# Up and gate projections with both halves of x in one 512-column product, a bank per 128 channels

## What is computed

```python
def sq_relu_mlp(h, w1, w2):                      # D_FF = 4096
    z = jax.nn.relu(jnp.einsum('bsd,df->bsf', h, w1))
    return jnp.einsum('bsf,fd->bsd', z * z, w2)
...
h = h + sq_relu_mlp(rmsnorm(h, norm_mlp[layer]), mlp_w1[layer], mlp_w2[layer])
...
def swiglu(x, w_gate, w_up, w_down):             # D_FF_2 = 2816
    return (jax.nn.silu(x @ w_gate) * (x @ w_up)) @ w_down
...
h = h + 0.5 * swiglu(rms_norm(h, ffn1_norm[l]), ffn1_w_gate[l], ffn1_w_up[l], ffn1_w_down[l])
```

## Time and profile before

| | |
|---|---|
| median of 3 runs | 1067.23 us (1067.21 to 1068.12) |
| the profiled execution's own time | 1068.05 us |
| its span, first to last instruction | 1066.3 us |
| TensorE busy | 1030.0 us, 97% |
| VectorE busy | 673.1 us, 63% |
| ScalarE busy | 485.1 us, 45% |
| GpSimd busy | 68.7 us, 6% |
| granted TensorE clock, mean | 0.989 of full |
| HBM traffic | 173 GB/s |

### The profile page before, as it was taken

One profiled execution on the slowest core, in us unless ns is written; L12 is line 12 of the kernel. 1 busy time (PEld: TensorE's weight loads), 2 busy tenths in 40 slices (PEclk: granted clock), 3 DMA queues, 4 the chain that ended last, 5 costly groups with the idle time before them and its releaser, 6 DMA issues.

```text
span 1066.3 us, 16323 instructions
## 1 busy us (share of the span) xinstructions
PE 1030.0 (97%) x6924; PEld 947.0 (89%) x6924; DVE 673.1 (63%) x825; ACT 485.1 (45%) x594; POOL 68.7 (6%) x62
## 2 busy tenths in 40 slices
PE   6999899999999959999999999999999999999997
PEld 5999799999989948999999999999998889999996
DVE  5577566555668796755665766555567666556554
ACT  5455354333436645443343644343355553434343
POOL 1200010000004641000000110000010010000000
PEclk9999999999999989999999999999999999999999
DMA  9953326655655423755656385655543335655611
GB/s 347 328 169 119 119 92 224 193 167 197 196 172 191 132 80 126 250 198 168 199 187 190 127 274 193 196 188 188 192 141 124 119 99 199 234 195 163 198 40 40
DMA packets 121814, 185.26 MB, mean 174 GB/s; under 512 B 3034, under 2 KB 100494, under 8 KB 121614
## 3 DMA queue, kind: packets, MB, share of 16 engines
q1 hardware_dynamic: 119760, 177.22, 50.6%
q0 software_dynamic: 1808, 6.93, 1.8%
q10 hardware_dynamic: 174, 0.08, 0.0%
HBM read 183.14 MB, written 1.07 MB: 173 GB/s over the span
## 4 chain that ended last, share of the span: by engine, by line
PE 82%; DVE 3%; ACT 2%; issue 1%; POOL 0%; POOLq 0%; DVEq 0%; ACTq 0%
PE bank L1233 31%; PE bank L1209 15%; PE bank L1211 15%; PE bank L1212 15%; PE bank L1259 1%; DVE w_lo L612 1%; PE bank L1380 1%; PE bank L1366 0%; DVE work L952 0%; PE bank L1535 0%; ACT w_hi L330 0%; PE bank L1537 0%; PE bank L1536 0%; PE bank L1488 0%; PE bank L1487 0%
## 5 line engine op out<-in xcount | busy, mean ns | idle before, releaser
L612 DVE TENSOR_TENSOR w_lo<-raw,w_hi 128x2048 fp32r<-128x2048 f32 x167 | 381.6, 2289 | 189.4 <-ACT w_hi L330 189.4
L1209 PE MATMUL bank<-xT_hi,w_hi 128*128 128x256 f32 x1520 | 435.2, 286 | 0.5 <-DVE w_lo L612 0.5
L1211 PE MATMUL bank<-xT_lo,w_hi 128*128 128x256 f32 x1520 | 429.9, 283 | 0.0
L1212 PE MATMUL bank<-xT_hi,w_lo 128*128 128x256 f32 x1520 | 429.8, 283 | 0.0
L330 ACT ACTIVATE w_hi<-raw 128x2048 fp32r<-128x2048 f32 x167 | 317.8, 1908 | 105.0 <-PE bank L1233 87.6
L1209 PEld LDWEIGHTS bank<-xT_hi,w_hi 128*128 128x128 f32 x1520 | 291.1, 192 | 4.1 <-issue 0.7
L1211 PEld LDWEIGHTS bank<-xT_lo,w_hi 128*128 128x128 f32 x1520 | 291.2, 192 | 2.3
L1212 PEld LDWEIGHTS bank<-xT_hi,w_lo 128*128 128x128 f32 x1520 | 291.1, 192 | 0.0
L1233 PE MATMUL bank<-w_hi,z_hi 128*128 128x512 f32 x440 | 142.3, 394 | 0.7 <-issue 0.7
L1233 PE MATMUL bank<-w_lo,z_hi 128*128 128x512 f32 x440 | 140.8, 390 | 0.0
L1233 PE MATMUL bank<-w_hi,z_lo 128*128 128x512 f32 x440 | 140.6, 390 | 0.0
(11 more groups left out here) (189 smaller groups left out, 805.7 us busy)
## 6 DMA issues: line engine op xcount, KB each, us to landing
raw<-in_w SPq DMA_DIRECT2D x64, 1024.0 KB, 5.3
raw<-in_f_gate SPq DMA_DIRECT2D x22, 1024.0 KB, 5.3
raw<-in_f_up SPq DMA_DIRECT2D x22, 1024.0 KB, 5.3
raw<-in_f_down SPq DMA_DIRECT2D x22, 1024.0 KB, 5.1
raw<-in_w_in SPq DMA_DIRECT2D x13, 1024.0 KB, 5.4
raw<-in_w_qkv SPq DMA_DIRECT2D x12, 1024.0 KB, 9.3
raw<-in_w_o SPq DMA_DIRECT2D x4, 1024.0 KB, 7.6
raw<-in_rec_w_o SPq DMA_DIRECT2D x4, 1024.0 KB, 5.8
```

The source lines that it names most:

```text
L612: e.tensor_tensor(w_lo[n % RING], raw[n % RAW], r32(w_hi[n % RING]), ALU.subtract).then_inc(lo_done, 1)
L1209: e.matmul(o, whi[:, k, cut], xT_hi[:, k, :], start=(k == 0 and b == 0), stop=False, skip_group_check=True)
L1211: e.matmul(o, whi[:, k, cut], xT_lo[:, k, :], start=False, stop=False, skip_group_check=True)
L1212: last = e.matmul(o, wlo[:, k, cut], xT_hi[:, k, :], start=False, stop=(k == KB - 1), skip_group_check=True)
```

## The change

x_hi and x_lo lie side by side in one tensor xT, and in the feed-forwards a new `u_wide` takes the place of `u_block`: one product of 512 columns puts w_hi by x_hi in the left half of a bank and w_hi by x_lo in the right, and w_lo by x_hi is added to the left. Each 128-channel half has a bank of its own: two banks per piece. `low_leaves` on ScalarE copies the right half of each to SBUF (`low`), `sums` on VectorE adds it to the left half. For nu = 1 the pieces alternate between banks 4, 5 and 6, 7; for nu = 2 gate has 4, 5 and up has 6, 7, and each piece waits for the sums of the piece before in its banks (`z_sum`).

Token factors: M0 and M1 have no `spread`, `diags`, POOL power or rms any more; since the square of r comes out as 1/var, VectorE's `reciprocal(down_scale, var)` gives a factor per token by which `add` scales the down projection's rows. In F1 and F2 only the gate is still multiplied by rms; the up half's factor, times 0.5, goes into `down_scale`. Their `spread` uses bank 1 and stands behind the last block of the second piece (up of pair 0), ahead of ups(1). The other stages keep `u_block` and rms; their semaphore counts are renumbered (`SPREAD`).

```diff
+SPREAD = {j: i + 1 for i, j in enumerate((L0, L1, F1, X2, F2))}
+SCALED = {L1: 1, F1: 2, X2: 3}
...
+    def sums(self, p, i):
+
+        return (self.g0 if self.nu == 1 else 2 * self.g0 - G_NU2) + self.nu * p + i + 1
+
+    def banks(self, p, i):
+
+        b = 4 + 2 * (p % 2 if self.nu == 1 else i)
+        return b, b + 1
...
-    xT_hi, xT_lo = sb("xT_hi", [P, KB, S], F32R), sb("xT_lo", [P, KB, S], F32R)
+    xT = sb("xT", [P, KB, 2, S], F32R)
+    xT_hi, xT_lo = xT[:, :, 0, :], xT[:, :, 1, :]
...
+        def low_leaves(f, p, i):
+            e.wait_ge(used, f.ups(p) + i + 1)
+            if f.sums(p, i) > 1:
+                e.wait_ge(z_sum, 2 * f.sums(p, i) - 2)
+            for b, n in enumerate(f.banks(p, i)):
+                e.activation(low[:, b * S:(b + 1) * S], bank[n][:, S:2 * S], ACT.Copy).then_inc(z_low, 1)
+
         def gate(f, p):
+            low_leaves(f, p, 0)
             e.wait_ge(z_g, f.g0 + p - G_NU2 + 1)
             e.activation(tmp[0], tmp[0], ACT.Silu).then_inc(z_s, 1)
 
         def z_finish(f, p):
             g, s = f.g0 + p, p % f.bufs
-            e.wait_ge(z_t if f.nu == 1 else z_f, g + 1)
+            low_leaves(f, p, f.nu - 1)
+            e.wait_ge(z_f, g + 1)
...
-            if f.nu == 1:
-                e.activation(z_hi[:, s, :], tmp[0], ACT.Square).then_inc(zhi_done, 1)
-            else:
-                e.activation(z_hi[:, s, :], tmp[2], ACT.Copy).then_inc(zhi_done, 1)
+            e.activation(z_hi[:, s, :], tmp[f.nu], ACT.Copy).then_inc(zhi_done, 1)
...
-            e.scalar_tensor_tensor(out=h[:, t, here], in0=acc[t][half], scalar=acc_scale[j], in1=h[:, t, here],
+            by = down_scale[:, t:t + 1] if j in SCALED else 1.0
+            e.scalar_tensor_tensor(out=h[:, t, here], in0=acc[t][half], scalar=by, in1=h[:, t, here],
...
-            if j != F1:
+            if j in SPREAD and j != F1:
                 diags(j)
...
+        def sums(f, p, i, t):
+
+            e.wait_ge(used, f.ups(p) + i + 1)
+            for b, n in enumerate(f.banks(p, i)):
+                e.wait_ge(z_low, 2 * f.sums(p, i) - 1 + b)
+                here = slice(b * S, (b + 1) * S)
+                e.tensor_tensor(t[:, here], bank[n][:, 0:S], low[:, here], ALU.add).then_inc(z_sum, 1)
+            e.wait_ge(z_sum, 2 * f.sums(p, i))
 
         def gate(f, p):
-            e.wait_ge(used, f.ups(p) + 1)
+            sums(f, p, 0, tmp[0])
...
-            e.tensor_tensor(pair(tmp[0]), pair(bank[4 + p % f.bufs * 2]), rms_pair(), ALU.mult).then_inc(z_g, 1)
+            e.tensor_tensor(pair(tmp[0]), pair(tmp[0]), rms_pair(), ALU.mult).then_inc(z_g, 1)
...
-                e.scalar_tensor_tensor(out=pair(t), in0=pair(src), scalar=0.0, in1=rms_pair(), op0=ALU.max,
-                                       op1=ALU.mult).then_inc(z_t, 1)
-                e.wait_ge(z_t, g_ + 1)
-                e.tensor_tensor(z, t, t, ALU.mult).then_inc(z_f, 1)
+                e.scalar_tensor_tensor(out=z, in0=t, scalar=0.0, in1=t, op0=ALU.max, op1=ALU.mult).then_inc(z_f, 1)
             else:
                 g, u, z = tmp
-                e.tensor_tensor(pair(u), pair(src), rms_pair(), ALU.mult).then_inc(z_t, 1)
+                sums(f, p, 1, u)
...
-            spread(f.j)
-            if f.nu == 2:
+            if f.nu == 1:
+
+                e.wait_ge(var_done, f.j + 1)
+                e.reciprocal(down_scale, var).then_inc(scale_done, 1)
+            else:
+                spread(f.j)
+                e.tensor_scalar(down_scale, rstd, 0.5, None, ALU.mult).then_inc(scale_done, 1)
                 gate(f, 0)
...
+        def u_wide(n, k, banks):
+
+
+            whi = w_hi[n % RING].rearrange("p (k c) -> p k c", k=KB)
+            wlo = w_lo[n % RING].rearrange("p (k c) -> p k c", k=KB)
+            for b, i in enumerate(banks):
+                cut = slice(b * P, (b + 1) * P)
+                e.matmul(bank[i], whi[:, k, cut], xT[:, k, :, :].rearrange("p b s -> p (b s)"), start=(k == 0),
+                         stop=False, skip_group_check=True)
+                last = e.matmul(bank[i][:, 0:S], wlo[:, k, cut], xT_hi[:, k, :], start=False, stop=(k == KB - 1),
+                                skip_group_check=True)
+            return last
...
-            def ups(p, between=None):
+            def ups(p):
                 for i in range(f.nu):
-                    if p >= f.bufs:
-                        e.wait_ge(z_g if f.nu == 2 and i == 0 else z_t,
-                                  f.g0 + p - f.bufs + 1 - (G_NU2 if f.nu == 2 and i == 0 else 0))
-                    if p == 1 and i == 1:
-                        e.wait_ge(rms_done, f.j + 1)
-                    u_piece(f.ups(p) + i, bank[4 + p % f.bufs * f.nu + i], between if i == 0 else None)
+
+                    before = p - 2 if f.nu == 1 else p - 1
+                    if before >= 0:
+                        e.wait_ge(z_sum, 2 * f.sums(before, i))
+                    u_piece(f.ups(p) + i, f.banks(p, i), None, u_wide)
...
-            first_u_piece(f.j, f.n0, bank[4])
+            first_u_piece(f.j, f.n0, f.banks(0, 0), u_wide)
             for i in range(1, f.nu):
-                u_piece(f.n0 + i, bank[4 + i])
+                u_piece(f.n0 + i, f.banks(0, i), {7: lambda: spread(f.j)}, u_wide)
             for p in range(1, f.pairs - 1):
-                ups(p, {3: lambda: spread(f.j)} if p == 1 else None)
+                ups(p)
+                z_ready(p - 1)
                 if p == 1:
                     for i in range(4):
                         e.matmul(bank[i][:, 0:2], zeros, zeros[:, 0:2], start=True, stop=False, skip_group_check=True)
-                z_ready(p - 1)
```

More of the change, by code:

```diff
@@ L230, in build @@
     MIX_BANK = {0: 0, 1: 2, 4: 0}
+    spread_bank = {L0: bank[7], L1: bank[7], F1: bank[1], X2: bank[7], F2: bank[1]}
     a_ = vec("a_param")
@@ L642, in turn @@
         def turn(j, n_next):
+            if j in SCALED:
+                e.wait_ge(scale_done, SCALED[j])
             for t in range(T):
@@ L653, in turn @@
             lo(n_next + 1)
[L654 removed]
+            if j in SPREAD and j != F1:
                 diags(j)
         def spread(j):
[L658 to L659 removed]
+            e.wait_ge(spread_done, SPREAD[j])
+            e.tensor_copy(rms, spread_bank[j][:, 0:S]).then_inc(rms_done, 1)
+        def sums(f, p, i, t):
[5 more added lines that the diff above has]
+            e.wait_ge(z_sum, 2 * f.sums(p, i))
         def gate(f, p):
[L662 removed]
+            sums(f, p, 0, tmp[0])
             if p == 0:
[L664 to L665 removed]
+                e.wait_ge(rms_done, SPREAD[f.j])
+            e.tensor_tensor(pair(tmp[0]), pair(tmp[0]), rms_pair(), ALU.mult).then_inc(z_g, 1)
         def z_finish(f, p):
             g_, s = f.g0 + p, p % f.bufs
[L669 to L670 removed]
             if f.nu == 1:
                 t, z = tmp[0], tmp[1]
[L673 to L675 removed]
+                sums(f, p, 0, t)
+                if p:
                     e.wait_ge(zhi_done, g_)
[L677 to L680 removed]
+                e.scalar_tensor_tensor(out=z, in0=t, scalar=0.0, in1=t, op0=ALU.max, op1=ALU.mult).then_inc(z_f, 1)
             else:
                 g, u, z = tmp
[L683 removed]
+                sums(f, p, 1, u)
                 e.wait_ge(z_s, g_ - G_NU2 + 1)
[L685 removed]
                 if p:
@@ L1090, in vector @@
         e.wait_ge(in_norm_last, 16)
+        e.wait_ge(scale_done, 4)
         for t in range(T):
@@ L1097, in vector @@
                 here = slice(half * HALF, (half + 1) * HALF)
-                e.scalar_tensor_tensor(out=h[:, t, here], in0=acc[t][half], scalar=0.5, in1=h[:, t, here],
-                                       op0=ALU.mult, op1=ALU.add).then_inc(last_h, 1)
+                e.scalar_tensor_tensor(out=h[:, t, here], in0=acc[t][half], scalar=down_scale[:, t:t + 1],
+                                       in1=h[:, t, here], op0=ALU.mult, op1=ALU.add).then_inc(last_h, 1)
                 e.wait_ge(last_h, 2 * t + half + 1)
@@ L1214, in u_block, with u_piece @@
             return last
-        def u_piece(n, dst, between=None):
+        def u_wide(n, k, banks):
[8 more added lines that the diff above has]
+            return last
+        def u_piece(n, dst, between=None, block=u_block):
             split(n)
             for k in range(KB):
-                mm = u_block(n, k, dst)
+                mm = block(n, k, dst)
                 if k == KB - 1:
@@ L1284, in closing_tokens, with first_u_piece @@
             d_part(n2, lhs2, 1, (0, 1), (1,), last=True).then_inc(used, 1)
-        def first_u_piece(j, n, dst):
+        def first_u_piece(j, n, dst, block=u_block):
             split(n)
```

40 lines of the change are left out of this document (18 added, 22 removed).

## The result

The changed kernel takes 1070.63 us (median of 20 runs, 1068.27 to 1071.70); the kernel before, in the same comparison, 1067.92 us (20 runs, 1064.55 to 1068.65). The ratio is 1.0028 with a 95% interval of 1.0020 to 1.0035: **slower by 0.28%**, where 1062.6 us and a gain were forecast. The time is outside the predicted range. The profiled execution took 1070.22 us, its span is 2.1 us longer than before, and the mean granted clock is 0.986.

The account below looks back on a forecast made before the run. TensorE's own work was taken to bound the feed-forward stages. The terms summed to -4.6 us, from 1067.23 us (median) to 1062.6 us, with a range of 1055.5 to 1069.5.

Parts of the forecast that it names:

- part 1: Up pieces of the feed-forwards: a 512-column product replaces two of 256, saving 0.0117 us each of 1216 times, -14.2 us.
- the middle: Wide products' gain taken as -14.2 us, between bounds of 0 and -28 us.
- rival A: Narrow product behind every wide one: the wide product saves nothing, the time is 1076.8 us; chance 0.09.
- the half-way case: Over the whole kernel: savings of about half; chance 0.05.
- part 2: M0 and M1: two small products that spread rstd go, 0.45 us each time, -0.9 us.
- part 3: Up pieces: added ScalarE copies and VectorE sums lengthen the way out of a bank, all hidden, cover 3.3 us at least.
- part 4: Starts of F1 and F2: the spread moved forward makes TensorE wait, +4.7 us in F1 and +1.7 us in F2.
- Part 6: Behind F1's start: the idle time brings one fall of the granted clock, +1.7 us, bounds nothing and 3.4.
- part 5: Stage ends: longer waits at the last pairs, +1.3 us in F2, +0.9 in F1, +0.2 in M0 and M1.

Follow-up runs that it names:

- e3: Changed kernel with all 16 wide products of an up piece ahead of its 16 narrow ones, except each stage's first piece: 1062.48 us, ratio 0.9951 to the kernel before.
- e1: Changed kernel with each wide product taken apart into two of 256 columns, all else kept: 1076.36 us, ratio 1.0077 to the kernel before.
- e8: Kernel before the change with only the new M0 and M1 token factors, no wide products or new banks: 1066.22 us, ratio 0.9985.
- e4: Changed kernel with F1's and F2's spread back in the third piece and pair 0's copies and sums ahead of it: 1062.61 us, ratio 0.9954 to the kernel before.
- e2: Changed kernel with the two wide products of each block k ahead of its two narrow ones: 1062.94 us, ratio 0.9948 to the kernel before.

## Why the prediction was wrong

**The step that failed is part 1's term**: "1216 x 0.0117 = -14.2 us", and in it the reason for taking the middle, that "pieces of 512 and of 256 already follow one another at every border, and the sum of the two pitches leaves nothing over". The two pitches were right, and e3 shows both in the changed kernel's own products. Wrong was to carry them into a stream in which the width changes after every product: the prediction itself said that no row shows it. A border has one change of width per 24 or 48 products; an up piece of the change has 32. The pair costs 0.353 us, not 0.3477: 6 ns are saved per pair in M0's stream where 11.7 were booked. By the distances of the down pieces this is 0.11 us for each of 32 pieces and 0.095 for each of 44, 7.7 us; by the times of e1 it is 5.7. The traces join the two: e1's four stages differ from the changed kernel's by 7.6 us, and 1.6 come back in L1, where the clock fell in one execution and not in the other.

The interval had the right ends (0 and -28), and rival A named the place, the narrow product behind the wide one, and its turning point, "less than 9.6 of the 14.2 us". With 5.7 to 7.7 the sign turned. But A was priced at its end, nothing saved, and the half-way case had 0.05. With no row that showed the alternation, everything between nothing and the full gain should have had a good share of the chances, and the range should have reached above 1070. Part 1 was 14.2 of the 25.6 us that the terms come to without regard to sign.

The Trainium skill (TensorE: Matmul & The Clock Gate, "Wait — 56ns, not 53.3ns?") puts the part beyond the columns at about 2.5 ns per product, by which the wide product would gain 3.0 us, an estimate. The measurement decides: e1 to e3 gives 13.9 us for it, 11.4 ns per removed product, so the trace's 12 ns stand for a stream of one width. With the widths in alternation the gain is 5.7 us by the times, 4.7 ns per product.

Point by point, from how much longer or shorter each stage is in the trace after than in the trace before (the stage drift; what the wide pieces save is taken out):

| step | forecast, us | measured, us | from |
|---|---|---|---|
| part 1, wide products | -14.2 | -7.7; by times -5.7 | distances of down pieces; e1 |
| part 2, spreads | -0.9 | -0.9 | e8's trace |
| part 3, way out of the banks | 0 | 0 | TensorE busy throughout |
| parts 4 and 6, F1's start | +6.4 | +6.7 | stage drift |
| part 4, F2's start | +1.7 | +1.6 | stage drift |
| part 5, F1's end | +0.9 | +0.6 | stage drift |
| part 5, F2's end | +1.3 | +1.0 | stage drift |
| part 5, ends of M0 and M1 | +0.2 | +0.2 | stage drift |

F1's row is from the last down products of M1 (597.27 before, 593.48 after) to F1's first down piece (624.60, 627.09): 33.61 us in place of 27.33, 6.3 more, plus the 0.4 us that four wide pieces save. With -7.7 in place of -14.2 the sum is +1.9 instead of -4.6 us, and the measured column adds up to +1.5; the two profiled executions are 1070.22 - 1068.05 = 2.2 us apart, the medians 2.7. So the one term makes up the miss and turns the sign.

**Part 4 was right**, and is what the other half of the sign hangs on: the two waits at F1's start came within 0.4 us of their forecast each, from the order on VectorE's queue. **Part 6 was right in kind**, a fall of the clock behind those waits and none at F2's start; e4 shows it go with them, and all five traces that have both waits have the fall. Its size was not: F1's +6.7 us is 4.05 us of waits, where 4.7 were booked, and so some 2.6 of lower clock (an estimate from these two) where 1.7 were; the two misses cancel, which is luck. And the row from which the 1.7 were taken, L1's fall behind a wait of 1.93 us, is missing in four of ten traces with the same wait. **Part 5** for F2's end: TensorE waits 1.2 us there for z_hi, against 1.6 forecast. **Part 2** was exact.

So the change has a gain of 13.9 us in its products, of which 8 are given back by their order, and it adds some 8 us of waits and lower clock at two places, which the moved spread makes and nothing in the wide product needs. Each of the two alone decides the sign: e3 without the one and e4 without the other are both 0.5% faster than before.

## What to carry to other kernels

When an edit changes what stands next to what in TensorE's stream, a pitch read from a stream of one shape is a bound, not an estimate: either there is a row with that alternation or the term keeps its whole interval in the chances. Products of one width belong together, since the same 32 products of a piece cost 8 us less over the kernel when grouped, and grouping lets the wait for the second operand move behind the first half of the work. A small step that is moved ahead in TensorE's program (here `spread`) has to be checked against the engine that feeds it; at F1's start, though not behind the single 1.25 us at F2's, the wait was paid with the clock on top. And where one trace shows a fall of the clock behind a short wait, look at a second execution before pricing it: in L1 it came in six traces of ten.

## What the runs showed of the hardware

That two pitches do not add up in alternation was not expected: 512 columns behind 512 take 0.227 us, 256 behind 256 take 0.120, and a pair in alternation 0.353 rather than 0.347, with the banks and the clock the same. In pairs of two (e2) the loss is all but gone. But the alternation has two paces, and 0.353 is only the usual one. In the changed kernel's trace all 64 up pieces that come after the first down piece of their stage run at 0.353 us per pair. The two pieces behind the stall at F1's start run at 0.347, from 617.82 on, once the clock is full again:

```profile
617.82 0.40 PE L1253 MATMUL bank<-xT,w_hi 128*128 128x512 f32 x1
...
618.17 0.39 PE L1253 MATMUL bank<-xT,w_hi 128*128 128x512 f32 x1
```

So do the first pieces of M0, M1 and F1. And one and the same piece can take either: the second of M0, whose program is the same in the changed kernel and in e4, at full clock in both traces. Its last 14 pairs took 4.95 us in the changed kernel, 0.354 each, and 4.85 us in e4, 0.346 each:

```profile
148.57 0.40 PE L1253 MATMUL bank<-xT,w_hi 128*128 128x512 f32 x1
...
153.52 0.40 PE L1253 MATMUL bank<-xT,w_hi 128*128 128x512 f32 x1
```

```profile
149.29 0.40 PE L1261 MATMUL bank<-xT,w_hi 128*128 128x512 f32 x1
...
154.14 0.40 PE L1261 MATMUL bank<-xT,w_hi 128*128 128x512 f32 x1
```

So the slow pace was seen only with this order of widths, but the order alone does not decide it. What chooses between them, and which part of TensorE costs the 6 ns, was not tested and stays open, as does the 1.7 us by which e3's and e4's gains do not add up.
